# Two attentions recast by head pairs: half-array products for scores and values, in place of one head at a time

## The chip, the cores and the metric

The kernel runs on one core of a Trainium2 chip. The time is that of one execution on the device in microseconds (us); lower is better. The engines are named as the profile names them: PE is TensorE's matmul side and PEld its weight loads, DVE is VectorE, ACT is ScalarE, POOL is GpSimd, SP issues DMAs.

## The reference, cut to what matters

The program is a first block (gated delta rule, gated feed-forward) and a second block of two transformer layers over T = 528 positions, padded inside the reference to whole blocks. The change touches the two attentions of the second block, each with 16 heads of 64 elements. The first one masks keys by a selection of 128 of them (called DSA in the code), the second one has a decay (called fox). What each computes per head:

```
s = jnp.einsum('bqhd,bshd->bhqs', q[:, q0:q1], k[:, :q1]) * scale
s = jnp.where(causal, s + decay, -jnp.inf)      # DSA: selected keys instead of decay
p = jax.nn.softmax(s, axis=-1)
outs.append(jnp.einsum('bhqs,bshd->bqhd', p, v[:, :q1]))
...
return o.reshape(B, T, B_W) @ w_out
```

In DSA four query heads share a key and value head.

## The kernel before, in words

Everything is float32. The 528 positions are cut into five chunks of C = 106 (the last has 104): `ROWS` holds the chunk sizes, `ENDS` the ends 106, 212, 318, 424, 528. Heads come in pairs p = 0 to 7, and a pair's 2 x 64 elements fill the 128 partitions of one tile of `pf`. Large products around the attentions (`products`, L518) take each weight and each activation apart into a high and a low part (`xbh`, `xbl` for the attention's output) and run as fp32r.

An attention is 80 units, one for each head h and query chunk t (`unit(n)`); `pe_attention` is called once for DSA and once for fox, and so are `act_attention`, `dve_attention` and `pool_attention`. One unit goes through these steps:

- `scores(n)`, L2176: queries as weights, keys moving, one PSUM bank of up to 512 columns, or two of 264 for the last chunk. Since a matmul contracts over all 128 partitions, POOL has copied each head's half of the queries into `qz`, whose other half is zero (L2148, L2149). Then a mask (L2184) or the decay and the diagonal mask (L2179, L2181) is added by a bf16 product into the same bank.
- `top(n)` on DVE (L2276, L2280): the row maximum; `exp(n)` on ACT (L2245): the exponential with its row sum.
- `turn(n)`, L2194: PE transposes the probabilities, 106 columns at a time; `out(n)` on ACT (L2255, L2257) copies them from PSUM to `ptr`.
- `values(n)`, L2207: `ptr` as weights (106 columns), the head's 64 value columns moving; the output is tokens x 64.

After a head, DVE divides by the row sums into `otok` (L2288). After a pair, `turn_output(p)` (L2216) transposes the output on PE, and DVE splits it into `xbh` and `xbl` (L2298, L2301). PE, ACT and DVE each follow their own written order, tied by semaphores. PE's loop is: scores of unit n + 3, turn of unit n, values of unit n - 1. An fp32 matmul of the program stands in the profile as two PE instructions, each with its own weight load; they are called passes below. A transposition and a bf16 product are one pass.

The program states for every matmul which part of PE's array it uses. Before, all matmuls of the attentions use the whole array of 128 rows by 128 columns. Elsewhere some use a part: L2326, which sums squares between the products of the fox projections, uses 32 columns of it, and L1204, in the delta rule, 32 rows.

Of the kernel before, what the change touches and what calls it, by code (L numbers as in the profile page):

```python
# [24 lines left out]
P = 128  # L25
# [126 lines left out]
def build_program(nc, io):  # L152
# [134 lines left out]
    qz = r2("qz", [P, 4, T])  # L287
# [29 lines left out]
    prob = [rt(f"prob{u}", [C, T]) for u in range(3)]  # L317
    ptr = [rt(f"ptr{u}", [C, T]) for u in range(2)]
    otok = rt("otok", [C, 2, NCH, P])
    rowmax = rt("rowmax", [C, 2 * NCH])  # L320
    rowsum = rt("rowsum", [C, 2, NCH])
    rowinv = rt("rowinv", [C, NCH])
# [19 lines left out]
    def sem(name):  # L342
        return nc.alloc_semaphore(name)
# [24 lines left out]
    def both(name):  # L368
# [27 lines left out]
    at_q, at_s, at_mx = sem("att_q"), sem("att_scores"), sem("att_max")  # L396
    at_p, at_pt, at_pte, at_o, at_oe, at_ot, at_of = map(sem, (
        "att_prob", "att_prob_turned", "att_prob_out", "att_value", "att_value_out", "att_turned",
        "att_stored"))
# [1520 lines left out]
    def pool_dsa(pool):  # L1920
# [47 lines left out]
        zero_halves(pool)  # L1968
# [73 lines left out]
    def zero_halves(pool):  # L2042
        for i in range(0, 4, 2):
            pool.memset(qz[64:P, i, :], 0.0)
            pool.memset(qz[0:64, i + 1, :], 0.0)

# [51 lines left out]
    def unit(n):  # L2098

        h, k = divmod(n, NCH)  # L2100
        return h, ORDER[k]

    def att_banks(fox):

        at, held, plan = 2 * (SEGS["fox_out" if fox else "dsa_out"].b0 % 2), {}, {}

        def take(key, n):
            nonlocal at
            mine = [(at + x) % 4 for x in range(n)]
            plan[key] = mine[0], [held[x] for x in mine if x in held]  # L2110
            held.update((x, key) for x in mine)
            at += n

        for n in range(UNITS):
            if n > 2 * NCH and n % (2 * NCH) == NCH:
                take(("out", n // (2 * NCH) - 1), 2)
            take(("unit", n), 2 if unit(n)[1] == 4 else 1)
        take(("out", HEADS // 2 - 1), 2)
        return plan

    TURN_BANK = {0: 4, 1: 5, 2: 6, 3: 4, 4: 5}
    TURN_BACK = {0: 2, 1: 2, 2: 3, 3: 3, 4: 2}

    def scale_of(n):
        h, t = unit(n)
        return q_scale[0:ROWS[t], t, h:h + 1]
# [13 lines left out]
    def pool_attention(pool, fox):  # L2140
        call = att_call("pool")
        for p in range(HEADS // 2):
            x = tile_at(pf, p + 16 if fox else p)
            if fox:
                pool.wait_ge(f_app, p + 9)
            if p >= 2:
                pool.wait_ge(at_s, UNITS * call + 2 * NCH * (p - 1))
            pool.tensor_copy(qz[0:64, 2 * (p % 2), :], x[0:64])  # L2148
            pool.tensor_copy(qz[64:P, 2 * (p % 2) + 1, :], x[64:P]).then_inc(at_q, 1)  # L2149

    def pe_attention(pe, fox, begun=None):
        call = att_call("pe")
        v = vtok if fox else vt2
        plan = att_banks(fox)

        def banks_free(key):
            b, held = plan[key]
            units = [n for what, n in held if what == "unit"]
            outs = [n for what, n in held if what == "out"]
            if units:  # L2160
                pe.wait_ge(at_p, UNITS * call + max(units) + 1)
            if outs:
                pe.wait_ge(at_of, HEADS // 2 * call + max(outs) + 1)
            return b

        def scores(n):
            h, t = unit(n)
            p, hh = divmod(h, 2)
            rows = ROWS[t]
            b = banks_free(("unit", n))  # L2170
            if n % (2 * NCH) == 0:
                pe.wait_ge(at_q, HEADS // 2 * call + p + 1)
            key = (p if fox else p // 4 + 8) * T
            for x, (o, c) in enumerate(pieces(ENDS[t])):
                s = ps[0:rows, b + x, 0:c]
                pe.matmul(s, qz[:, 2 * (p % 2) + hh, t * C:ENDS[t]], pf[:, key + o:key + o + c], start=True, stop=False)  # L2176
                if fox:
                    diagonal = o + c == ENDS[t]
                    mm = pe.matmul(s, headrow[:, h, 0:rows], decay_row[:, o:o + c], start=False, stop=not diagonal)  # L2179
                    if diagonal:  # L2180
                        mm = pe.matmul(ps[0:rows, b + x, c - rows:c], ident16[0:rows, 0:rows],  # L2181
                                       mask16[0:rows, 0, 0:rows], start=False, stop=True)
                else:
                    mm = pe.matmul(s, ident16[0:rows, 0:rows], mask16[0:rows, t, o:o + c], start=False, stop=True)  # L2184
            mm.then_inc(at_s, 1)

        def turn(n):
            t = unit(n)[1]
            rows = ROWS[t]
            pe.wait_ge(at_p, UNITS * call + n + 1)  # L2190
            if n >= TURN_BACK[t]:
                pe.wait_ge(at_pte, UNITS * call + n - TURN_BACK[t] + 1)
            for kb in range(t + 1):
                mm = pe.transpose(ps[0:ROWS[kb], TURN_BANK[t] + kb // 4, (kb % 4) * rows:(kb % 4 + 1) * rows],  # L2194
                                  prob[n % 3][0:rows, kb * C:ENDS[kb]], ident[0:rows, 0:rows])
            mm.then_inc(at_pt, 1)

        def values(n):
            h, t = unit(n)
            p, hh = divmod(h, 2)  # L2200
            rows = ROWS[t]
            pe.wait_ge(at_pte, UNITS * call + n + 1)
            if n % NCH == 0 and h:
                pe.wait_ge(at_oe, HEADS * call + h)
            col = (p if fox else p // 4) * P + 64 * hh
            for kb in range(t + 1):
                mm = pe.matmul(ps[0:rows, 7, t * 64:(t + 1) * 64], ptr[n % 2][0:ROWS[kb], kb * rows:(kb + 1) * rows],  # L2207
                               v[0:ROWS[kb], kb, col:col + 64], start=(kb == 0), stop=(kb == t))
            if n % NCH == NCH - 1:
                mm.then_inc(at_o, 1)  # L2210

        def turn_output(p):
            pe.wait_ge(at_oe, HEADS * call + 2 * p + 2)
            b = banks_free(("out", p))
            for t in range(NCH):
                mm = pe.transpose(ps[:, b + t // 4, (t % 4) * C:(t % 4) * C + ROWS[t]], otok[0:ROWS[t], p % 2, t, :],  # L2216
                                  ident[0:ROWS[t], 0:ROWS[t]])
            mm.then_inc(at_ot, 1)

        if fox:  # L2220
            pe.wait_ge(acc_free, SEGS["fox_out"].b0)
        for n in range(3):
            scores(n)
        if begun is not None:
            begun(pe)
        for n in range(UNITS):
# [7 lines left out]
        values(UNITS - 1)  # L2234
        turn_output(HEADS // 2 - 1)

    def act_attention(act, fox):
        call = att_call("act")
        plan = att_banks(fox)

        def exp(n):
            h, t = unit(n)
            w_, rows = ENDS[t], ROWS[t]
            act.wait_ge(at_mx, UNITS * call + n + 1)
            act.activation(as_psum(prob[n % 3][0:rows, 0:w_], w_), psum_cols(plan["unit", n][0], rows, w_), ACT.Exp,  # L2245
                           bias=rowmax[0:rows, n % (2 * NCH):n % (2 * NCH) + 1],
                           accum_out=rowsum[0:rows, h % 2, t:t + 1],
                           **({} if fox else {"scale": scale_of(n)})).then_inc(at_p, 1)

        def out(n):  # L2250
            t = unit(n)[1]
            rows = ROWS[t]
            w_ = min(t + 1, 4) * rows
            act.wait_ge(at_pt, UNITS * call + n + 1)
            last = act.activation(ptr[n % 2][:, 0:w_], ps[0:C, TURN_BANK[t], 0:w_], ACT.Copy)  # L2255
            if t == 4:
                last = act.activation(ptr[n % 2][0:rows, w_:w_ + rows], ps[0:rows, TURN_BANK[t] + 1, 0:rows], ACT.Copy)  # L2257
            last.then_inc(at_pte, 1)

        exp(0)  # L2260
        exp(1)
        for n in range(UNITS):
            if n + 2 < UNITS:
                exp(n + 2)
            out(n)

    def dve_attention(dve, fox):
        call = att_call("dve")
        plan = att_banks(fox)

        def top(n):
            t = unit(n)[1]
# [590 lines left out]
```

## Time and profile before

| what | value |
|---|---|
| time, median of 3 runs | 2951.91 us (2951.75 to 2953.01) |
| profiled execution, its own time | 2949.52 us |
| its span, first to last instruction | 2947.7 us |
| PE busy in the span | 2743.1 us (93%) |
| DVE, ACT, POOL busy | 1416.6, 1027.5, 1097.4 us |
| DSA attention, from first scores to last values | about 1624.7 to 1769.5 us |
| fox attention | about 2384.9 to 2527.9 us |

The two attentions are some 288 us of the span together. In the profile a matmul's duration includes the way through the array; how fast matmuls follow each other is seen from starts alone, so the text below subtracts starts. A row with x8 is eight instructions in a run, with the start of the first.

### The profile page before, as it was taken

What the parts mean: (1) busy time and instruction counts of PE and PEld (TensorE: products, weight loads), DVE (VectorE), ACT (ScalarE), POOL (GpSimd) and SP (SyncE); (2) the same over time, 40 slices, a digit from 0 to 9 for tenths busy, and PEclk for the clock granted to TensorE, in tenths of its full rate; (3) what the DMA queues carried; (4) which work ended last, traced back from release to release, by engine and by line L of the source; (5) the groups of instructions that cost most, each with busy time, mean ns of one, the idle gap of its engine ahead of it and who ended that gap; (6) DMA issues with size and microseconds to landing.
All of it is one profiled execution on the core that took longest, in us unless ns stands there. A gap on an engine that the chain in (4) does not pass through costs nothing.

```text
span 2947.7 us, 48050 instructions
## 1 busy us (share of the span) xinstructions
PE 2743.1 (93%) x17591; PEld 2400.7 (81%) x17591; DVE 1416.6 (48%) x2151; ACT 1027.5 (35%) x1762; POOL 1097.4 (37%) x588
## 2 busy tenths in 40 slices
PE   6986888889999999999898899999999999999998
PEld 6964788868987778888778779999998988777876
DVE  2563565633213663323779556345366224555433
ACT  4762222233243332222433563212233255422221
POOL 3422433324444434444437104444444310344443
PEclk8997989999999999999999999999999999999999
DMA  3210000012333333333212002232322210133332
GB/s 97 90 50 7 11 10 12 11 59 89 92 89 93 93 94 92 93 93 94 86 43 65 1 1 81 91 86 86 93 86 79 65 30 1 58 93 93 93 93 93
DMA packets 88858, 197.89 MB, mean 67 GB/s; under 512 B 38140, under 2 KB 40238, under 8 KB 88728
## 3 DMA queue, kind: packets, MB, share of 16 engines
q1 hardware_dynamic: 84964, 192.72, 22.2%
q10 hardware_dynamic: 3764, 3.38, 0.4%
q8 instruction: 88, 1.44, 0.2%
q14 instruction: 42, 0.34, 0.0%
HBM read 192.24 MB, written 3.82 MB: 67 GB/s over the span
## 4 chain that ended last, share of the span: by engine, by line
issue 44%; PE 17%; POOL 12%; DVE 4%; ACT 1%; DVEq 1%; POOLq 1%; ACTq 0%
POOL wl L482 12%; PE ps L518 9%; PE ps L2176 2%; PE ps L2207 2%; DVE work L2076 1%; DVE top L2073 1%; PE ps L2194 1%; PE ps L1823 1%; PE ps L2326 1%; PE ps L2335 1%; ACT prob L2245 0%; POOLq L130 0%; DVE rowmax L2276 0%; PE ps L2179 0%; PE ps L893 0%
## 5 line engine op out<-in xcount | busy, mean ns | idle before, releaser
L482 POOL TENSOR_TENSOR wl<-wraw,wh 128x1024 fp32r<-128x1024 f32 x353 | 876.3, 2483 | 1289.8 <-ACT wh L474 1289.7
L474 ACT ACTIVATE wh<-wraw 128x1024 fp32r<-128x1024 f32 x353 | 372.6, 1055 | 576.7 <-PE ps L518 488.8
L518 PE MATMUL ps<-xah,wh 128*128 128x264 f32 (+1 forms) x2672 | 500.1, 328 | 25.6 <-ACT xah L847 14.2
L518 PE MATMUL ps<-xah,wl 128*128 128x264 f32 (+1 forms) x2672 | 488.3, 323 | 0.0
L518 PE MATMUL ps<-xal,wh 128*128 128x264 f32 (+1 forms) x2672 | 486.7, 322 | 0.0
L518 PEld LDWEIGHTS ps<-xah,wh 128*128 128x128 f32 x2672 | 405.7, 189 | 79.6 <-issue 23.2
L518 PEld LDWEIGHTS ps<-xah,wl 128*128 128x128 f32 x2672 | 404.0, 189 | 41.4 <-issue 0.8
L518 PEld LDWEIGHTS ps<-xal,wh 128*128 128x128 f32 x2672 | 402.3, 188 | 40.7
L666 DVE TENSOR_TENSOR res<-res,stage 128x512 f32 (+3 forms) x112 | 81.7, 729 | 440.8 <-ACT stage L582 440.8
L518 PE MATMUL ps<-xbh,wh 128*128 128x264 f32 (+1 forms) x1392 | 275.3, 338 | 13.5 <-POOL wl L482 12.9
L518 PE MATMUL ps<-xbh,wl 128*128 128x264 f32 (+1 forms) x1392 | 269.7, 333 | 0.0
L518 PE MATMUL ps<-xbl,wh 128*128 128x264 f32 (+1 forms) x1392 | 269.5, 333 | 0.0
L518 PEld LDWEIGHTS ps<-xbh,wh 128*128 128x128 f32 x1392 | 218.3, 189 | 48.5 <-POOL wl L482 16.4
L582 ACT ACTIVATE stage<-ps 128x512 f32<-128x512 f32 (+1 forms) x136 | 81.9, 603 | 466.9 <-PE ps L518 466.8
L518 PEld LDWEIGHTS ps<-xbh,wl 128*128 128x128 f32 x1392 | 217.7, 188 | 27.6
L518 PEld LDWEIGHTS ps<-xbl,wh 128*128 128x128 f32 x1392 | 217.5, 188 | 27.4
L659 DVE TENSOR_SCALAR xbh<-stage 128x512 f32 (+3 forms) x102 | 145.3, 1424 | 18.2 <-issue 16.6
L2176 PE MATMUL ps<-pf,qz 128*104 128x264 f32 (+4 forms) x384 | 125.3, 413 | 24.6 <-ACT prob L2245 13.7
L2276 DVE TENSOR_REDUCE rowmax<-ps 106x1 f32<-106x106 f32 (+4 forms) x160 | 77.7, 488 | 127.2 <-PE ps L2181 70.2
L661 DVE TENSOR_TENSOR xbl<-stage,xbh 128x512 f32 (+3 forms) x102 | 116.4, 1142 | 14.6
L1196 PE MATMUL ps<-xq,ob 106*106 106x106 f32 x480 | 65.4, 301 | 59.8 <-DVE xq L1499 39.9
L1196 PEld LDWEIGHTS ps<-xq,ob 106*106 106x106 f32 x480 | 60.7, 213 | 62.2 <-DVE xq L1499 41.5
(337 smaller groups left out, 3198.9 us busy)
## 6 DMA issues: line engine op xcount, KB each, us to landing
wraw<-in_w SPq DMA_DIRECT2D x353, 512.0 KB, 3.6
res<-in_x SPq DMA_DIRECT2D x4, 528.0 KB, 5.7
res<-in_x ACTq DMA_DIRECT2D x1, 2048.0 KB, 7.9
out<-res SPq DMA_DIRECT2D x1, 2048.0 KB, 6.9
block_in<-mt SPq DMA_DIRECT2D x120, 4.0 KB
xq<-block_out SPq DMA_DIRECT2D x120, 8.0 KB
block_out<-yy SPq DMA_DIRECT2D x20, 56.0 KB
cossin<-in_cossin ACTq DMA_DIRECT2D x1, 528.0 KB
```

The costliest lines, as they stand in the source:

```text
L474: act.activation(wh[:, s * DM:(s + 1) * DM], wraw[:, s * DM:(s + 1) * DM], ACT.Copy).then_inc(hi_done, 1)
L482: pool.tensor_tensor(wl[:, s * DM:(s + 1) * DM], wraw[:, s * DM:(s + 1) * DM], wh[:, s * DM:(s + 1) * DM].bitcast(F32), ALU.subtract).then ...
L518: mm = pe.matmul(ps[:, 2 * s + h, 0:width], ws[:, s * DM + kk * P:s * DM + (kk + 1) * P], x[:, at:at + width], start=(h not in [o[0] for o ...
L582: act.activation(shaped(out(j, u), live), acc(b, live=live), func, **more).then_inc(acc_free, 1)
L659: dve.tensor_scalar(hi, x, 1.0, None, ALU.mult)
L661: return dve.tensor_tensor(lo, x, hi.bitcast(F32), ALU.subtract)
L666: return dve.tensor_tensor(r, r, live_stage(u) if live else stage_at(u), ALU.add)
L1196: mm = pe.matmul(out_[:, sl], lhs(r, sl), rhs(r, sl), start=True, stop=True)
L1823: mm = pe.matmul(ps[0:ROWS[t], 4 + 2 * (n % 2) + x, 0:c], ix_zero[:, 2 * (m % 2) + hh, C * t:ENDS[t]], pf[:, 16 * T + o:16 * T + o + c], s ...
L2176: pe.matmul(s, qz[:, 2 * (p % 2) + hh, t * C:ENDS[t]], pf[:, key + o:key + o + c], start=True, stop=False)
L2207: mm = pe.matmul(ps[0:rows, 7, t * 64:(t + 1) * 64], ptr[n % 2][0:ROWS[kb], kb * rows:(kb + 1) * rows], v[0:ROWS[kb], kb, col:col + 64], s ...
L2276: most = dve.tensor_reduce(m, psum_cols(plan["unit", n][0], rows, w_), AX.X if w_ <= 512 else AX.XY, ALU.max, negate=True)
```

## The change

Both attentions are now 48 parts instead of 80 units. A part is a pair of heads and a query chunk; the last chunk is cut into key blocks 0 to 2 and 3 to 4, so that no part is wider than 424 columns. There are six parts per pair.

- Scores: no `qz`. Head 0 of the pair contracts over rows 0 to 63 of the array and head 1 over rows 64 to 127, each into a bank of its own. The mask and decay products still use the whole array.
- Values: the operands change places. The 64 value columns are the weights, and the turned probabilities move (106 columns); head 0 writes output partitions 0 to 63 and head 1 64 to 127, each from its half of the array's columns. The output comes out as heads x tokens, as the next stage needs it, so `otok` and `turn_output` go.
- The inverse row sums must then lie along the columns: `spread_sums` multiplies them, as 64 equal weight columns, with the identity matrix. ACT copies the result to `rowspread`, DVE multiplies (`store`), and POOL makes `xbh` and `xbl`.
- The copies of the turned probabilities are shared: ACT takes the first two key blocks of a part, DVE the rest. One `tensor_reduce` gives the maxima of both heads.

```diff
@@ parts @@
+    PARTS_OF = ((0, 0, 1), (1, 0, 2), (2, 0, 3), (3, 0, 4), (4, 0, 3), (4, 3, 2))
+    SCORE_BANK, TURN_BANK, VALUE_BANK = 0, 4, 6
@@ pool_attention @@
-            pool.tensor_copy(qz[0:64, 2 * (p % 2), :], x[0:64])
-            pool.tensor_copy(qz[64:P, 2 * (p % 2) + 1, :], x[64:P]).then_inc(at_q, 1)
+            x = ofull[p % 2][:, :]
+            pool.wait_ge(at_oe, 2 * (PAIRS * call + p + 1))
+            pool.tensor_copy(tile_at(xbh, p), x)
+            pool.drain()
+            pool.tensor_tensor(tile_at(xbl, p), x, tile_at(xbh, p).bitcast(F32), ALU.subtract).then_inc(at_of, 1)
@@ pe_attention @@
+        def scores(j):
...
+            if j >= 2:
+                pe.wait_ge(at_p, 2 * (ALL * call + j - 1))
...
+            for hh in range(2):
+                half = slice(64 * hh, 64 * hh + 64)
+                pe.matmul(ps[0:rows, b + hh, 0:hi - lo], pf[half, q0:q0 + rows], pf[half, k0 + lo:k0 + hi],
+                          start=True, stop=False)
...
-            for kb in range(t + 1):
-                mm = pe.matmul(ps[0:rows, 7, t * 64:(t + 1) * 64], ptr[n % 2][0:ROWS[kb], kb * rows:(kb + 1) * rows],
-                               v[0:ROWS[kb], kb, col:col + 64], start=(kb == 0), stop=(kb == t))
+        def spread_sums(p, i):
...
+                for hh in range(2):
+                    mm = pe.matmul(ps[64 * hh:64 * hh + 64, b, at:at + rows],
+                                   rowinv[0:rows, p % 2, t, hh:hh + 1].broadcast_to([rows, 64]),
+                                   ident[0:rows, 0:rows], start=True, stop=True)
...
+        def values(j):
...
+            for i, (kb, nk) in enumerate(groups(j)):
+                copied(pe, SLOT["turn", j, i], call)
+                for x in range(nk):
+                    for hh in range(2):
...
+                        mm = pe.matmul(ps[64 * hh:64 * hh + 64, VALUE_BANK + t // 4, at:at + rows],
+                                       v[0:n, kb + x, col:col + 64], ptr[TURN["turn", j, i] % 4][0:n, at2:at2 + rows],
+                                       start=(kb + x == 0), stop=(kb + x == t))
...
-        for n in range(UNITS):
-            if n + 3 < UNITS:
-                if n + 3 > 2 * NCH and (n + 3) % (2 * NCH) == NCH:
-                    turn_output((n + 3) // (2 * NCH) - 1)
-                scores(n + 3)
-            turn(n)
-            if n:
-                values(n - 1)
+        for j in range(ALL):
+            p, k = divmod(j, NS)
+            if j + 2 < ALL:
+                scores(j + 2)
+            turn(j)
+            if k == 4:
+                spread_sums(p, 0)
+            if k == 0 and p:
+                spread_sums(p - 1, 1)
+            if j and k != 4:
+                values(j - 1)
+            if k == 3:
+                values(j)
@@ dve_attention @@
+        def store(p, i):
...
+            dve.tensor_tensor(ofull[p % 2][:, lo:hi], ps[:, VALUE_BANK + i, 0:hi - lo], rowspread[:, lo:hi], ALU.mult
+                              ).then_inc(at_oe, 1)
```

PE's rows in the middle of the DSA attention before, from the scores of the fourth chunk of one head to the first scores of the next pair; `ps` is PSUM, `prob` the probabilities, `ptr` their transposed copies, and an x says how many matmuls of the program:

```order
L2176 MATMUL ps<-pf,qz 106x424
L2184 MATMUL ps<-mask_155,ident_156 106x424
L2194 MATMUL ps<-ident,prob_185 106x106
L2207 MATMUL ps<-vtok_dsa,ptr_187 104x64 x5
L2176 MATMUL ps<-pf,qz 104x264
L2184 MATMUL ps<-mask_155,ident_156 104x264
L2176 MATMUL ps<-pf,qz 104x264
L2184 MATMUL ps<-mask_155,ident_156 104x264
L2194 MATMUL ps<-ident,prob_183 106x106 x2
L2207 MATMUL ps<-vtok_dsa,ptr_186 106x64
L2216 MATMUL ps<-ident,otok 128x106 x4
L2216 MATMUL ps<-ident,otok 128x104
```

The same place in the changed kernel, where scores are L2193, masks L2205, turns L2223, spreads of the inverse sums L2234 and values L2254:

```order
L2193 MATMUL ps<-pf 106x424 x2
L2205 MATMUL ps<-mask_155,ident_156 106x424 x2
L2223 MATMUL ps<-ident,prob_183 106x106 x4
L2254 MATMUL ps<-ptr_186,vtok_dsa 64x106 x2
L2193 MATMUL ps<-pf 104x318 x2
L2205 MATMUL ps<-mask_155,ident_156 104x318 x2
L2223 MATMUL ps<-ident,prob_184 106x106 x6
L2254 MATMUL ps<-ptr_187,vtok_dsa 64x106 x4
```

The row of output transpositions is gone, every score and value product stands in twos, and PE goes through three uses of the array in each part: L2193 by row halves, L2205 and L2223 whole, L2254 (and L2234) by column halves. Further on in the same pair, at the fourth chunk and the last, the changed kernel has:

```order
L2223 MATMUL ps<-ident,prob_182 106x106 x8
L2254 MATMUL ps<-ptr_188,vtok_dsa 64x106 x4
L2254 MATMUL ps<-ptr_185,vtok_dsa 64x106 x2
L2254 MATMUL ps<-ptr_186,vtok_dsa 64x106 x4
L2254 MATMUL ps<-ptr_187,vtok_dsa 64x106 x4
L2193 MATMUL ps<-pf 106x106 x2
L2205 MATMUL ps<-mask_155,ident_156 106x106 x2
L2223 MATMUL ps<-ident,prob_183 106x104 x6
L2234 MATMUL ps<-ident,rowinv 64x106 x8
```

Here the values of the part that has just been turned (`ptr_186`, `ptr_187`) follow in the same round, behind those of the part before (`ptr_188`, `ptr_185`), and the spread takes the place of values in the round of the last chunk.

## Rows read from the trace of the kernel before

**Rows 1.** The page, section 5: the costliest group

```profile
L482 POOL TENSOR_TENSOR wl<-wraw,wh 128x1024 fp32r<-128x1024 f32 x353 | 876.3, 2483 | 1289.8 <-ACT wh L474 1289.7
```

**Rows 2.** Windows, one pair each of DSA and fox: PE, PEld, DVE, ACT, POOL, clock

```profile
1658.30:1676.00 17.70, 15.96 (x132) 13.44 (x131) 9.51 (x29) 10.64 (x33) 1.25 (x2) 1.00 0.00 1
2413.30:2430.40 17.10, 16.28 (x144) 13.94 (x143) 7.66 (x19) 9.86 (x32) 1.25 (x2) 1.00 0.01 2
```

**Rows 3.** Chain of waits in DSA, one same event three pairs apart

```profile
1640.53 0.88 ACT prob L2245 x2
...
1693.70 0.88 ACT prob L2245 x2
```

**Rows 4.** Chain of waits in fox, one same event four pairs apart

```profile
2413.33 0.53 PE ps L2207 x6
...
2481.73 0.53 PE ps L2207 x6
```

**Rows 5.** Timeline of PE in DSA: start, us, what, shapes, number

```profile
1758.43 0.61 PE L2194 MATMUL ps<-ident,prob 104*106 104x104 f32 x5
1758.88 0.88 PE L2207 MATMUL ps<-vtok_dsa,ptr 106*106 106x64 f32 x8
1759.59 0.91 PE L2176 MATMUL ps<-pf,qz 128*106 128x424 f32 x2
1760.34 0.34 PE L2184 MATMUL ps<-mask,ident 106*106 106x424 bf16 x1
1760.53 0.25 PE L2194 MATMUL ps<-ident,prob 106*106 106x106 f32 x1
```

**Rows 6.** Timeline of PEld, the weight loads, in the same stretch

```profile
1758.79 0.82 PEld L2207 LDWEIGHTS ps<-vtok_dsa,ptr 106*106 106x106 f32 x8
1759.54 0.27 PEld L2176 LDWEIGHTS ps<-pf,qz 128*106 128x106 f32 x2
```

**Rows 7.** Waits in the DSA attention: who for whom, us, times, longest

```profile
ACT ptr L2255 <- PE ps L2194: 36.5, 62, 0.9
...
PE ps L2176 <- ACT prob L2245: 8.1, 7, 1.2
```

**Rows 8.** Timeline of PE around L2326, which uses 32 columns

```profile
2239.58 0.77 PE L518 MATMUL ps<-xal,wh 128*128 128x264 f32 x5
2240.28 1.06 PE L2326 MATMUL ps<-fox_sq,win 128*16 128x264 f32 x4
2241.27 1.24 PE L518 MATMUL ps<-xah,wh 128*128 128x264 f32 x8
2242.34 1.13 PE L518 MATMUL ps<-xah,wl 128*128 128x264 f32 x8
2243.31 0.29 PE L518 MATMUL ps<-xal,wh 128*128 128x264 f32 x1
```

**Rows 9.** Timeline of PE around L1204, which uses 32 rows

```profile
449.64 1.69 PE L1204 MATMUL ps<-mt,ones 16*128 16x424 f32 x4
451.26 0.91 PE L1196 MATMUL ps<-rr,xq 106*106 106x128 f32 x6
```

**Rows 10.** Groups by shape in the DSA attention: busy us, mean ns, idle

```profile
L2245 ACT ACTIVATE prob<-ps,rowmax,q_scale 106x424 f32<-106x424 f32 x16 | 11.3, 705 | 8.2 <-DVE rowmax L2280 8.2
L2276 DVE TENSOR_REDUCE rowmax<-ps 106x1 f32<-106x424 f32 x16 | 9.6, 600 | 21.6 <-PE ps L2184 21.6
L2255 ACT ACTIVATE ptr<-ps 106x424 f32<-106x424 f32 x16 | 8.4, 526 | 2.3 <-PE ps L2194 2.3
```

**Rows 11.** Timeline where DSA begins

```profile
1623.24 0.62 POOL L2148 COPY qz<-pf 64x528 f32<-64x528 f32 x1 [7.59 <-DVEq L418]
1624.67 0.66 PE L2176 MATMUL ps<-pf,qz 128*106 128x106 f32 x2 [10.62 <-POOL qz L2149]
```

**Rows 12.** Timeline where fox ends

```profile
2527.45 0.68 PE L2216 MATMUL ps<-ident,otok 106*128 106x106 f32 x5 [0.85 <-DVE otok L2288]
2527.90 3.26 PE L518 MATMUL ps<-xbh,wh 128*128 128x512 f32 x7
```

More of the change, by code:

```diff
@@ new lines, in groups, with att_slots @@
+    def groups(j):
+        _, _, _, kb, nk = part(j)
+        return [(kb + i, min(2, nk - i)) for i in range(0, nk, 2)]
+    def att_slots():
+        slots, act, dve = [], 0, 0
+        for j in range(ALL):
+            p, k = divmod(j, NS)
+            mine = [("turn", j, i) for i in range(len(groups(j)))]
+            if k == 4:
+                mine.append(("spread", p, 0))
+            if k == 0 and p:
+                mine.append(("spread", p - 1, 1))
+            if j == ALL - 1:
+                mine.append(("spread", p, 1))
+            for key in mine:
+                on_dve = key[0] == "turn" and key[2] == 1
+                act, dve = (act, dve + 1) if on_dve else (act + 1, dve)
+                slots.append((key, on_dve, dve if on_dve else act))
+        return slots, act, dve
@@ new lines, in build_program, with slot_bank, copied, spread_tiles @@
+    SLOTS, ACT_COPIES, DVE_COPIES = att_slots()
+    SLOT = {key: n for n, (key, _, _) in enumerate(SLOTS)}
+    TURNS = [key for key, _, _ in SLOTS if key[0] == "turn"]
+    TURN = {key: n for n, key in enumerate(TURNS)}
+    def slot_bank(n):
+        return TURN_BANK + n % 2
+    def copied(e, n, call):
+        _, on_dve, count = SLOTS[n]
+        if on_dve:
+            e.wait_ge(at_td, DVE_COPIES * call + count)
+        else:
+            e.wait_ge(at_ta, ACT_COPIES * call + count)
+    def spread_tiles(i):
+        return range(4) if i == 0 else range(4, NCH)
@@ L2128, in pool_fox, with values_done @@
+    def values_done(j):
+        return sum(len(groups(i)) for i in range(j + 1))
+    ALL_GROUPS = values_done(ALL - 1)
     def pool_fox(pool):
@@ L2153, in pe_attention @@
         v = vtok if fox else vt2
[L2154 to L2176, printed above, removed]
+        def scores(j):
+            p, k, t, _, _ = part(j)
+            rows, (lo, hi) = ROWS[t], key_range(j)
+            b = SCORE_BANK + 2 * (j % 2)
+            if j >= 2:
+                pe.wait_ge(at_p, 2 * (ALL * call + j - 1))
+            if fox and k == 0:
+                pe.wait_ge(f_app, p + 9)
+            q0 = (p + 16 if fox else p) * T + t * C
+            k0 = (p if fox else p // 4 + 8) * T
+            for hh in range(2):
[3 more added lines that the diff above has]
+            for hh in range(2):
+                s = ps[0:rows, b + hh, 0:hi - lo]
@@ L2212, in turn_output, with slot_free @@
[L2212 to L2218, printed above, removed]
+        def slot_free(key):
+            n = SLOT[key]
+            if n >= 2:
+                copied(pe, n - 2, call)
+            return slot_bank(n)
@@ L2237, in act_attention @@
     def act_attention(act, fox):
         call = att_call("act")
[L2239 to L2258, printed above, removed]
+        def exp(j):
+            p, k, t, _, _ = part(j)
+            rows, (lo, hi) = ROWS[t], key_range(j)
+            act.wait_ge(at_mx, ALL * call + (j + 2 if k == 4 else j + 1))
+            if j >= 3:
+                act.wait_ge(at_t, turned_by(j - 3))
+            for hh in range(2):
+                h = 2 * p + hh
+                act.activation(prob[j % 3][0:rows, hh, 0:hi - lo], ps[0:rows, SCORE_BANK + 2 * (j % 2) + hh, 0:hi - lo],
+                               ACT.Exp, bias=rowmax[0:rows, (p * NCH + t) % 3, 0, hh:hh + 1],
+                               accum_out=rowsum[0:rows, p % 2, k, hh:hh + 1],
+                               **({} if fox else {"scale": q_scale[0:rows, t, h:h + 1]})).then_inc(at_p, 1)
@@ new lines, in turned_by, with out @@
+        def turned_by(j):
+            return len(SLOTS) * call + SLOT["turn", j, len(groups(j)) - 1] + 1
+        def out(j):
+            _, _, t, _, _ = part(j)
+            kb, nk = groups(j)[0]
+            n = TURN["turn", j, 0]
+            act.wait_ge(at_t, len(SLOTS) * call + SLOT["turn", j, 0] + 1)
+            wait(act, at_v, ALL_GROUPS * call + n - 3 if n >= 4 else 0)
+            w_ = 2 * nk * ROWS[t]
+            act.activation(ptr[n % 4][:, 0:w_], ps[0:C, slot_bank(SLOT["turn", j, 0]), 0:w_], ACT.Copy
+                           ).then_inc(at_ta, 1)
@@ L2260, in act_attention, with spread_out @@
+        def spread_out(p, i):
+            n = SLOT["spread", p, i]
+            act.wait_ge(at_t, len(SLOTS) * call + n + 1)
+            wait(act, at_oe, 2 * (PAIRS * call + p) - 1 + i)
+            lo, hi = (0, 4 * C) if i == 0 else (4 * C, T)
+            act.activation(rowspread[:, lo:hi], ps[:, slot_bank(n), 0:hi - lo], ACT.Copy).then_inc(at_ta, 1)
         exp(0)
         exp(1)
[L2262 to L2265, printed above, removed]
+        for j in range(ALL):
+            p, k = divmod(j, NS)
+            out(j)
+            if k == 4:
+                spread_out(p, 0)
+            if k == 0 and p:
+                spread_out(p - 1, 1)
+            if j + 2 < ALL and k != 2:
+                exp(j + 1 if k == 3 else j + 2)
+            if k == 3:
+                exp(j + 2)
@@ L2316, in build_program @@
+        for j in range(ALL):
+            p, k = divmod(j, NS)
+            if j + 2 < ALL:
+                top(j + 2)
+            if len(groups(j)) > 1:
+                out(j)
+            if k == 3:
+                invert(p, 0)
+            if k == 4:
+                store(p, 0)
+            if k == 5:
+                invert(p, 1)
+            if k == 0 and p:
+                store(p - 1, 1)
+        store(PAIRS - 1, 1)
     FOX = SEGS["fox"].b0
```

207 lines of the change are left out of this document (100 added, 107 removed).

## The prediction, made before the changed kernel ran

> **What bounds the kernel now.** I read the page first: PE is busy nearly all of the span, so a stage's time is PE's unless it waits. Then the windows, cut to one pair of heads. In DSA a pair takes 17.7 us, of which PE is busy 15.96; in fox 17.1 and 16.28 [rows 2]. DVE and ACT are busy 7.7 to 10.6 us of it. The clock is 1.00 in both, the 2.4 GHz level. The chain of waits gives the period exactly: 53.17 us for three pairs of DSA, 17.72 each, and 68.40 for four pairs of fox, 17.10 each [rows 3, 4]. The wait list of DSA has ACT waiting for turns by the dozen, and PE waiting for an exponential only 8.1 us in seven of its waits [rows 7]. PE sets both attentions, with small stalls.
>
> The timeline gives the price of a PE pass as the distance of starts [rows 5, 6]:
> - scores, 424 columns: 1759.59 to 1760.34, 0.75 for two passes, 0.375 each or 0.885 ns a column;
> - mask in bf16, 424 columns: 0.19, and 0.05 for 106;
> - turn: 1758.43 to 1758.88, 0.45 for five, 0.09 each;
> - values: only 64 columns move, but each pass takes 0.75/8 = 0.094 on PEld, from 1758.79 to 1759.54. The load of 106 fp32 weight columns sets it. By its columns a load of 64 would take 0.057, an estimate.
>
> A pair has 3176 score columns (two heads of 106 + 212 + 318 + 424 + 528) in two passes: 5.62 us. Masks 1.42, 30 turns 2.70, 60 value passes 5.63, five output turns 0.45. Sum 15.8 us; fox has ten diagonal masks more, 16.3. What is left of the periods, 1.9 and 0.8 us, is stall.
>
> **The change, part by part, for a pair.**
>
> Entering and leaving a part of the array. L2326 stands between fp32r products of 0.97/8 = 0.121 us each [rows 8]. Five of them from 2239.58 would end at 2240.19; L2326 starts 0.09 later. Its four passes of 264 columns, 0.222 to 0.234 each, end at 2241.17 to 2241.21; the next product starts 0.06 to 0.10 later, and its first eight take 1.07 instead of 0.97, since the first load lies open. L1204, in 32 rows, takes 1.62 us for four passes of 424 columns that make 1.50 at the rate above [rows 9]. So each change of use costs about 0.09 us and lays one weight load open. The new loop changes three times a round (columns to rows for the scores, rows to whole for masks and turns, whole to columns for values or spread), 18 times a pair: 18 x 0.09 = 1.62 us, plus the open loads. PE did none of this in the attentions before.
>
> The Trainium skill states the same (TensorEngine Tiling, "Key Properties"): changing the tiling mode drains TensorE. It speaks against this change, and the trace agrees with about 0.09 us. If switches were free, the sum would be 1.62 us a pair lower.
>
> Scores: 1588 columns per pass over the six parts, four passes (two heads, two each). What the trace of before does not show is two halves of the array at work together; no instruction there uses a second tile. Bounds: no overlap, four passes in a row; full overlap, two. Within a head the two passes share a half, so with matmuls started in program order A1, A2, B1, B2, only A2 and B1 can run together: three passes, 3 x 1.405 = 4.22, and six open loads of 0.094, 0.56. I take 4.8 (bounds 3.4 and 6.2; before 5.6).
>
> Masks: 1.42, and six open bf16 loads of 0.05: 1.7. Turns: 30, 2.7, unchanged.
>
> Values: still 60 passes. Now 106 columns move, 0.094 each, and 64 are loaded, 0.057. Alone a pass costs 0.094, as before: turning the operands around gains nothing by itself. With the halves overlapping, PE is held by the loads: 0.057. I take that, since it is the nearest row to a pass whose stream is hidden: 60 x 0.057 = 3.4, and six open loads, 0.3 (bounds: 0.047, half a stream, and 0.094; so 2.8 to 5.6).
>
> Spreads: five chunks, two heads, two passes, 20 x 0.057 = 1.1 (to 1.9). They replace output turns of 0.45: the product is fp32 and costs two passes where a turn costs one.
>
> Sum: 4.8 + 1.7 + 2.7 + 3.7 + 1.1 + 1.6 = 15.6 us, fox 16.1. The gain from overlap, about 1.4 in scores and 2.2 in values against passes in a row, is nearly eaten by switches, open loads and spreads.
>
> Other engines. ACT's 10.6 us a pair [rows 2] gain two short exponentials and the copy of the spread and lose a few copies of about 0.5 [rows 10]; DVE gives up splits and gets those copies, with half as many, wider maxima: the widest, 2 x 424 columns, is under twice 0.60 [rows 10]. Both stay near 10 of 16. POOL's subtraction of 528 columns is 2.48 x 528/1024 = 1.3 us [rows 1], its copy no more: idle time of POOL covers it; only at the end of an attention is it late, and there the first block of products leaves the last input tile for last.
>
> Stalls. `values` of the fourth chunk stands right behind its own turn. It needs the copy, 0.53 [rows 10] to 0.6 on DVE, while PE does values of the third chunk, six blocks, 12 passes x 0.057 plus a switch, 0.8: mostly covered, 0.2 open. Behind it on PE stand the next pair's scores. The other wait is scores of part j + 2 for the exponentials of part j. From the end of a part's scores to the end of its two exponentials the widest takes 1.2 + 0.16 + 2 x 0.9 = 3.2 us; PE has one and a half rounds, 3.9, to do meanwhile. Short rounds at a pair's start will stall. I take 1.1 us for DSA and 1.0 for fox, between the 0.8 and 1.9 of now.
>
> Periods: 16.7 us in DSA against 17.72, 8 x -1.0 = -8; 17.1 in fox against 17.10, nothing. The queries' copy into `qz` before the first scores of DSA, 1623.24 to 1624.67 [rows 11], goes: -1.3. At each end PE no longer waits for `otok`, 0.85 of idle time before the last output turns [rows 12], but waits some 0.3 for its last copies: -1.0 in all. Total -10.3. The profiled execution is 2949.5 us, 2.4 below the median of the runs; -10 from the median gives **2942 us**.
>
> **The rivals.**
>
> *Loads in program order (slower, 0.28).* A load in rows 6 starts as the matmul before it starts. If this is order, and not the one spare place for weights, then B's load waits for A2 to start: in the values a cycle of four passes is 0.094 + 0.057 + 0.094 + 0.057 = 0.30, 0.075 a pass, and each part's scores lose another load. 80 x 0.018 + 5 x 0.09 = 1.9 us a pair. PE then waits less, 0.6: 15.6 + 1.9 + 0.6 = 18.1 in DSA, 18.6 in fox. 8 x (0.4 + 1.5) = +15, less 2.3 at the ends, less up to 6 if short stalls vanish: +7 to +13, 2962 us. It decides once a pass of values is over some 0.065 us. For it speaks that no load in the trace is ever ahead of a matmul not yet started; against it, that in whole-array use the trace can't show it.
>
> A page rules near this: the Trainium skill (TensorE: Matmul & The Clock Gate, "The mechanism") has loads overlap running matmuls only where the row groups differ, and the column halves share all rows. Rows 6 contradict it in its bare form, since loads of 128 rows run under matmuls of 128 rows all through.
>
> *No overlap of halves (slower, 0.10).* Scores 6.2, values 5.6 + 0.3, spreads 1.9: 20.0 us with 0.6 of stall, and 20.5: +18 and +27, 2995 us. Nothing in the profile speaks against it. The Trainium skill does (TensorEngine Tiling, "Key Properties"): tiles load and multiply in parallel.
>
> *The halves run by themselves (faster, 0.16).* If each half takes up its passes without regard to the other's, scores are two passes, 3.4, and values 0.047: 13.4 us of work. Then the chain from scores to exponentials (3.2 us for two rounds of 2.3) and ACT start to hold: 15.4 to 15.7 us. 8 x (-2.2 - 1.5) = -30, 2920 us.
>
> *The new wait is not covered (0.08).* Copies queued behind two exponentials on ACT (1.8 us) come late for values of the fourth chunk: 1 us in each of 16 pairs, 2958 us.
>
> **How the numbers follow.** Chances: forecast 0.36, the rivals 0.28, 0.10, 0.16, 0.08, something else 0.02. The forecast's own range is 2934 to 2950. From 2914 (the independent halves) to 2975 (program order, with its upper bound) all but no overlap is in; that leaves about 0.13 out. A measurement can tell about 0.2%, 6 us. Faster by more: most of the forecast, 0.29, and the independent halves, 0.16: 0.45. Within: 0.18. Slower by more: 0.37.
>
> **What the changed profile would show.** Starts of values (L2254) 0.057 us apart right, 0.075 program order, 0.094 no overlap. Scores of 424 columns: from the first start to the mask 1.1 to 1.2 us right, 1.5 no overlap, 0.75 independent. PEld idle about 0.09 before each change of use. Pairs at 16.7 and 17.1 us. PE's wait for copies before L2254 small, POOL late nowhere. The prediction is wrong above all if the halves overlap more or less than that, or if a switch between halves costs more than the 0.09 of a part in 32 columns.

## The result, and the profile after

The changed kernel takes 2907.68 us (median of 4 runs, 2903.69 to 2911.96), the kernel before 2952.06 us beside it (4 runs, 2951.75 to 2953.01). The ratio is 0.985, 95% interval 0.9838 to 0.9862: 44 us faster, far more than the forecast 10, and 6 us below the range. The profiled execution took 2911.96 us, the slowest of the four; its span is 2910.1 us, so 37.6 of the 44 us can be looked for in it.

Windows of the changed kernel, one pair of DSA and one of fox; columns as in [rows 2]:

```profile
1685.05:1699.22 14.17, 13.53 (x149) 9.24 (x147) 7.47 (x20) 10.51 (x33) 1.93 (x2) 1.00 0.01 2
2430.41:2444.61 14.20, 13.77 (x158) 9.73 (x156) 6.74 (x15) 9.48 (x33) 1.93 (x2) 1.00 0.00 1
```

A pair now lasts 14.17 and 14.20 us, 3.55 and 2.90 less than the periods of [rows 3, 4]. PE still fills it (13.53 and 13.77), so PE still sets both attentions; PE itself has less to do. The chain of waits, here POOL's last step of a pair in DSA and in fox, says the same, 14.17 to 14.25 a pair:

```profile
1678.57 1.31 POOL xbl L2175
1692.82 1.30 POOL xbl L2175
1706.99 1.31 POOL xbl L2175
...
2438.40 1.31 POOL xbl L2175
2452.60 1.30 POOL xbl L2175
```

PE's timeline in the middle of a DSA pair. To be read by starts, and beside [rows 5]: scores L2193, mask L2205, turns L2223, spreads L2234, values L2254.

```profile
1688.78 0.76 PE L2254 MATMUL ps<-ptr,vtok_dsa 106*64 106x104 f32 x12
1689.46 0.79 PE L2193 MATMUL ps<-pf 64*106 64x318 f32 x4
...
1690.99 0.53 PE L2254 MATMUL ps<-ptr,vtok_dsa 106*64 106x104 f32 x8
1691.46 0.96 PE L2193 MATMUL ps<-pf 64*106 64x424 f32 x4
1692.35 0.56 PE L2205 MATMUL ps<-mask,ident 106*106 106x424 bf16 x2
1692.75 0.53 PE L2223 MATMUL ps<-ident,prob 106*106 106x106 f32 x4
1693.21 0.40 PE L2254 MATMUL ps<-ptr,vtok_dsa 106*64 106x106 f32 x4
1693.54 0.79 PE L2193 MATMUL ps<-pf 64*104 64x318 f32 x4
```

Scores of 424 columns: 1691.46 to 1692.35, 0.89 for four passes and the change of use behind them. Without that change (0.09) it is 0.80, near the 0.75 that the prediction had named for independent halves and far from its own 1.1 to 1.2. Values that stand between turns and scores: twelve passes take 0.68 to the next scores, four 0.33, so eight more cost 0.35, or 0.044 each, where the prediction had 0.057.

Four narrow windows on the values (L2254) just after 1680.94, PE busy and, as (x..), the passes under way in each (a pass stays under way for 0.25 to 0.31 us, so the number grows):

```profile
1680.94:1681.03 0.09, 0.08 (x2) 1.00 0.00 0
1681.03:1681.12 0.09, 0.09 (x4) 1.00 0.00 0
1681.12:1681.21 0.09, 0.09 (x6) 1.00 0.00 0
1681.21:1681.30 0.09, 0.09 (x8) 1.00 0.00 0
```

Every 0.09 us two more passes are under way, not one: each half runs at the 0.094 of [rows 6] for itself, side by side with the other. That is the price of 0.045 a pass.

What waits now, DSA attention (us in total, times, longest):

```profile
POOL xbh L2173 <- DVE ofull L2378: 114.7, 8, 31.8
DVE rowmax L2343 <- PE ps L2205: 39.4, 41, 2.8
...
ACT ptr L2308 <- PE ps L2223: 11.2, 18, 1.5
...
PE ps L2234 <- ACT ptr L2308: 3.6, 8, 0.6
PE ps L2193 <- ACT prob L2292: 2.8, 7, 1.5
...
PE ps L2254 <- DVE ptr L2361: 0.5, 2, 0.3
```

POOL, DVE and ACT wait for PE. PE waits about 0.43 us a pair for the copy ahead of the spreads and 0.2 for exponentials; values wait for their copies twice in the stage.

Where it is not faster: the start of fox. Timeline of PE there, and windows of the first two pairs and of the stretch at the low clock:

```profile
2367.83 1.40 PE L2193 MATMUL ps<-pf 64*106 64x318 f32 x4 [3.58 <-ACT prob L2292]
```

```profile
2361.98:2384.12 22.14, 18.57 (x111) 11.96 (x111) 5.51 (x10) 11.66 (x39) 0.00 (x0) 0.59 0.00 1
2384.12:2402.01 17.89, 17.63 (x158) 12.35 (x156) 6.83 (x15) 8.70 (x29) 1.93 (x2) 0.75 0.00 1
2366.00:2390.00 24.00, 21.91 (x130) 14.68 (x131) 5.88 (x11) 10.40 (x35) 0.00 (x0) 0.50 0.00 1
```

PE stands idle for 3.58 us until the first exponentials are there, and then the granted clock is 0.50, the 1.2 GHz level, for 24 us and more. The first two pairs, from first scores to first scores, take 22.14 and 17.89 us, 11.6 us more than two steady pairs. (Before, the first fox pair took 17.08 us with a wait of 2.30 in it, as long as a steady one.)

The stages, from first scores to the first product of what follows, before from [rows 11, 12] and the table of times before, after from the starts 1627.68, 1746.44, 2361.98 and 2491.74 of these lines:

```profile
1627.68 0.69 PE L2193 MATMUL ps<-pf 64*106 64x106 f32 x4 [9.17 <-DVEq L417]
...
1746.44 1.12 PE L517 MATMUL ps<-xbh,wh 128*128 128x264 f32 x7
...
2491.05 0.40 PE L2234 MATMUL ps<-ident,rowinv 104*64 104x104 f32 x4 [0.47 <-DVE rowinv L2371]
2491.25 0.56 PE L2254 MATMUL ps<-ptr,vtok 106*64 106x104 f32 x8
2491.74 1.89 PE L517 MATMUL ps<-xbh,wh 128*128 128x512 f32 x7
```

DSA took about 144.8 us and now takes 118.8 (-26); fox took 143.0 and now takes 129.8 (-13).

### The profile page after: what moved, and what is told of

Its sections match the earlier page's. It is cut to its first block, busy times and chain, and to the rows that moved or that the text cites. A ratio compares the mean times of both kernels' runs of the same rounds, so it can differ in the third digit from the quotient of the medians.

```text
span 2910.1 us, 48627 instructions
## 1 busy us (share of the span) xinstructions
PE 2717.8 (93%) x17831; PEld 2342.6 (80%) x17831; DVE 1397.0 (48%) x2063; ACT 1023.8 (35%) x1762; POOL 1106.1 (38%) x584
## 3 DMA queue, kind: packets, MB, share of 16 engines
q8 instruction: 90, 1.47, 0.2%
## 4 chain that ended last, share of the span: by engine, by line
issue 53%; POOL 13%; PE 5%; DVE 3%; POOLq 3%; DVEq 1%; ACT 0%; ACTq 0%
POOL wl L481 12%; PE ps L517 3%; POOLq L2166 2%; DVE work L2069 1%; DVE top L2066 1%; PE ps L1822 1%; POOL xbl L2175 1%; POOLq L130 0%; POOLq L2174 0%; PE ps L892 0%; PE ps L880 0%; POOLq L2163 0%; PE ps L2193 0%; DVEq L618 0%; DVEq L2067 0%
## 5 line engine op out<-in xcount | busy, mean ns | idle before, releaser
L517 PE MATMUL ps<-xah,wh 128*128 128x264 f32 (+1 forms) x2672 | 500.4, 328 | 24.0 <-ACT xah L846 14.2
L658 DVE TENSOR_SCALAR xbh<-stage 128x512 f32 (+3 forms) x102 | 146.3, 1434 | 18.9 <-issue 17.3
L2343 DVE TENSOR_REDUCE rowmax<-ps 106x2 f32<-106x212 f32 (+2 forms) x96 | 68.0, 708 | 96.0 <-PE ps L2202 48.8
L2173 POOL CAST xbh<-ofull 128x528 fp32r<-128x528 f32 x16 | 10.0, 625 | 233.9 <-DVE ofull L2378 233.9
```

What stands on the lines that cost most here:

```text
L517: mm = pe.matmul(ps[:, 2 * s + h, 0:width], ws[:, s * DM + kk * P:s * DM + (kk + 1) * P], x[:, at:at + width], start=(h not in [o[0] for o ...
L658: dve.tensor_scalar(hi, x, 1.0, None, ALU.mult)
L2343: most = dve.tensor_reduce(rowmax[0:rows, n, 1 if k == LAST4 else 0, :], ps[0:rows, b:b + 2, 0:hi - lo], AX.X, ALU.max, negate=True)
```

## The experiments

Three readings of the result are weighed. The main one: the halves of the array run wholly by themselves, in scores and in values, and that is what the forecast missed; 0.09 us a change of use holds. Rival one: only one of the two overlaps, and the rest comes from work that left. Rival two: the changes of use cost nothing, and the halves overlap only in part. (The expectations letter their own theories anew each time.) The last experiments look at the fox start instead. Steady pairs are taken from the chain of waits, POOL's last step of a pair. All experiments start from the changed kernel.

**Values in one half.** Both heads' values go through column half 0 and are summed there, so nothing can overlap; the second head's output is left out.

```diff
-                        mm = pe.matmul(ps[64 * hh:64 * hh + 64, VALUE_BANK + t // 4, at:at + rows],
+                        mm = pe.matmul(ps[0:64, VALUE_BANK + t // 4, at:at + rows],
...
-                                       start=(kb + x == 0), stop=(kb + x == t))
+                                       start=(kb + x == 0 and hh == 0), stop=(kb + x == t and hh == 1))
```

> Both heads' value products go to the column half 0 and are summed there, so the second head's output is left out; number, shapes and order of the instructions and all changes of use of the array stay. Theory A, the two halves run side by side and that is the gain: 30 passes of 0.09 us a pair come back on the path, 16 x 2.7 = +43, 2951 us. Theory B, the forecast's partial overlap limited by loads: +14 to +28. Theory C, the gain is from fewer waits between the engines: within 5 us of the changed kernel.

Measured: 2945.83 us (10 runs, 2941.98 to 2949.25), ratio to the kernel before 0.998 (0.997 to 0.9989); pairs of 16.36 and 16.87 us, +2.19 and +2.67. Timeline of PE, the longest run of values in a DSA pair:

```profile
1703.52 2.76 PE L2254 MATMUL ps<-ptr,vtok_dsa 106*64 106x106 f32 x28
1706.20 0.44 PE L2193 MATMUL ps<-pf 64*106 64x106 f32 x4
```

and the same 28 passes in the changed kernel, in fox:

```profile
2485.79 1.50 PE L2254 MATMUL ps<-ptr,vtok 106*64 106x106 f32 x28
2487.22 0.75 PE L2223 MATMUL ps<-ident,prob 104*106 104x104 f32 x6
```

2.68 us against 1.43, less 0.09 for the change behind each: 0.0925 and 0.048 a pass. Without the overlap of the values the kernel is 38 us slower, near the +43 of both halves side by side and outside the +14 to +28 of a partial overlap.

**Scores in one half.** Both heads contract over rows 0 to 63, so the second head's scores are those of the first.

```diff
-                half = slice(64 * hh, 64 * hh + 64)
+                half = slice(0, 64)
```

> Both heads' scores contract over rows 0 to 63, so the second head's scores are those of the first head; all else as it is. Theory A: two more passes of each part's width in a row, 2 x 1.32 us a pair, +42, 2950 us, less what stalls take up. Theory B (program order, only the second pass of head 0 beside the first of head 1): +21. Theory C: within 5 us.

Measured: 2981.98 us (4 runs, 2970.44 to 2985.97), ratio 1.0095 (1.0068 to 1.0122); pairs of 16.74 and 16.84, +2.57 and +2.64. Timeline of PE, the scores of 424 columns:

```profile
1731.11 1.67 PE L2193 MATMUL ps<-pf 64*106 64x424 f32 x4
1732.71 0.56 PE L2205 MATMUL ps<-mask,ident 106*106 106x424 bf16 x2
```

1.60 us where the changed kernel has 0.89: four passes of 0.375 and one change of use. The pairs make 16 x 2.6 = 42 us, as expected. Rival one falls: each of the two overlaps costs about 40 us when it is taken away. A pair with neither would take 14.17 + 2.19 + 2.57 = 18.9 us in DSA and 14.20 + 2.67 + 2.64 = 19.5 in fox, an estimate, and so more than before (17.72 and 17.10): the overlap carries the whole gain. The run lost not 42 but 74 us. The windows of its profile show where most of the other 32 lie:

```profile
1618.00:1706.00 88.00, 81.11 (x376) 52.31 (x378) 26.53 (x71) 31.03 (x92) 3.84 (x4) 0.50 0.00 1
1706.00:1740.00 34.00, 32.87 (x308) 22.83 (x304) 15.16 (x40) 20.78 (x63) 3.85 (x4) 0.99 0.01 1
```

The granted clock is 0.50 for 88 us at the start of DSA, and pairs there take up to 29.6 us. Why this order of work keeps the clock low for so long is not settled.

**Values head by head.** Within a group all passes of head 0, then all of head 1, instead of taking turns.

```diff
-                for x in range(nk):
-                    for hh in range(2):
+                for hh in range(2):
+                    for x in range(nk):
```

> Values of a group of two key blocks are written head by head (four passes of half 0, then four of half 1) instead of alternating. Theory A, each half takes up its own matmuls as they come: no change, at most +3 us. Theory B, matmuls start in the order of the program and overlap only with the neighbour: of eight passes only two overlap in each group, +25 to +30 us.

Measured: 2909.81 us (4 runs, 2902.45 to 2913.52), ratio 0.9852 (0.9833 to 0.9871); pairs of 14.22 and 14.31, +0.05 and +0.11. Its 28 passes of values in a row:

```profile
2412.25 1.55 PE L2254 MATMUL ps<-ptr,vtok 106*64 106x106 f32 x28
2413.72 0.44 PE L2193 MATMUL ps<-pf 64*106 64x106 f32 x4
```

They take 1.47 us with the change behind them, where taking turns took 1.43. Even four passes of one half in a row leave the other half running: a half takes up its passes ahead of matmuls that were issued earlier for the other. Starts in program order, on which two of the prediction's cases rested, would have cost 25 to 30 us by the expectation; 2 were measured.

**More changes of use**, and **the same product without them.** Between masks and turns of each part stands a tiny product of 64 columns: in the first kernel in a column half, which adds two changes a part, in the second in the whole array, which adds none. (The second one's weights are 128 columns, the first one's 64.)

```diff
+                if i == 0:
+                    pe.matmul(ps[0:64, b, 0:64], ident[:, 0:64], ident[:, 0:64], start=True, stop=True)
```

```diff
+                if i == 0:
+                    pe.matmul(ps[:, b, 0:64], ident[:, :], ident[:, 0:64], start=True, stop=True)
```

> Between masks and turns of each part stands one more tiny product of 64 columns by a column half, so the use of the array changes twice more (96 parts). By 0.09 us a change with the loads laid open and two passes: 0.39 us a part, +38 us against the changed kernel, and 17 more than the control in the whole array. If changes cost nothing by themselves: no more than the control.

> The control: the same tiny product over the whole array, so the use does not change there. Two passes with loads of 128 columns, 0.107 us each: 0.21 us a part, +20 us. The difference of the two is the price of two changes in each of 96 parts, 17 us by 0.09 each.

Measured: with changes 2958.18 us (10 runs, 2944.03 to 2967.25; ratio 1.0012, 0.9994 to 1.0031), pairs of 16.15 and 16.57; without 2923.88 (4 runs, 2918.2 to 2932.06; 0.9914, 0.9891 to 0.9936), pairs of 15.02 and 15.52. Timelines of PE around one such product (L2221), with changes and then without:

```profile
1738.18 0.56 PE L2205 MATMUL ps<-mask,ident 106*106 106x424 bf16 x2
1738.68 0.33 PE L2221 MATMUL ps<-ident 128*64 128x64 f32 x2
1738.94 0.57 PE L2225 MATMUL ps<-ident,prob 106*106 106x106 f32 x4
```

```profile
1738.48 0.56 PE L2205 MATMUL ps<-mask,ident 106*106 106x424 bf16 x2
1738.88 0.33 PE L2221 MATMUL ps<-ident 128*128 128x64 f32 x2
1739.05 0.53 PE L2225 MATMUL ps<-ident,prob 106*106 106x106 f32 x4
```

The mask takes 0.50 to the next start with a change and 0.40 without, the product 0.26 and 0.17. Per pair the difference is 1.13 and 1.05 us for 12 changes, 0.09 each. Rival two falls. The 0.10 ahead of the product is free of the difference in weights; in the 0.09 behind it the wider loads of the control are not told apart. (The times differ by 34 us, twice the 17 of the pairs; the kernel with changes has a window around its fox start, 2360 to 2425, at a mean clock of 0.72.)

**Products in the wait at the fox start.** Fifteen products whose result is not used stand where PE waits for the first exponentials.

```diff
+            pe.wait_ge(f_app, 16)
+            for _ in range(15):
+                pe.matmul(ps[:, VALUE_BANK, 0:HT], ident[:, :], pf[:, 0:HT], start=True, stop=True)
```

> In the changed kernel fox begins with a wait of PE for the first exponentials, 3.5 us, and the clock then stands at 0.50 for some 27 us; its first two pairs take 22.2 and 17.9 us instead of 14.2. Here 15 useless products of 264 columns fill that wait (they write a bank that the values write over later). Theory: the halved clock took most of what fox gained less than DSA. It expects the clock at 1.00 all through fox's start, the second pair at 14.2 us, and 2898 us (8 to 11 less than the changed kernel). Rival: the start is slow because of ACT's copies and table load, and the clock costs nothing: no change, within 2 us.

Measured: 2906.36 us (4 runs, 2902.11 to 2909.65), ratio 0.9845 (0.9829 to 0.9862). In its profile the low clock is gone, windows over the start of fox:

```profile
2362.00:2380.00 18.00, 17.85 (x140) 13.12 (x139) 5.41 (x11) 11.20 (x35) 0.00 (x0) 1.00 0.01 4
2380.00:2400.00 20.00, 19.14 (x225) 13.53 (x222) 8.82 (x21) 13.70 (x49) 1.93 (x2) 1.00 0.00 1
```

but the median moved by only 1.3 us, within the spread, where 8 to 11 had been expected. So it was run again beside an unchanged copy, with one more kernel that also fills the idle time before DSA (24 such products into bank 4, ahead of the barrier and behind ACT's last copy of the values).

> The changed kernel once more, word for word, to stand beside the next two on the same chip. Its first fox pairs took 22.15 and 17.89 us instead of 14.20 in the profiled execution, under a granted clock of 0.50 for 27.3 us. Theory A (that spell belongs to most executions): 2904 to 2912 again. Theory B (the spell comes in some executions and not in others): single times scattered over the same range of some 8 us, and a profile in which the spell may be absent.

> The first experiment again (15 useless products of 264 columns in TensorE's wait at the start of the fox attention). Theory A (the clock spell belongs to most executions of the changed kernel and the products take it away): 5 to 8 us below the unchanged kernel beside it, and first pairs of about 17.8 and 14.2 us. Theory B (the spell is not in every execution, or moves elsewhere): within 2 us of it.

> As the one before, and 24 useless products of 264 columns (about 0.29 us each, some 7 us) in TensorE's idle stretch of 9 us before the first scores of the DSA attention. If a granted clock of 0.50 at the start of the DSA attention comes from that idle stretch, the first DSA pair falls from 14.8 us to about 14.2 and the stretch at 0.50 is gone or shorter: 1 to 3 us below the experiment beside it. If the clock there is set by something else, no difference, and if the products end late, up to 1 us more.

Measured, all on one chip: unchanged 2908.41 us (4 runs, 2906.93 to 2911.95; ratio 0.9851, 0.9836 to 0.9866), fox filled 2903.78 (5 runs, 2900.52 to 2905.41; 0.983, 0.9817 to 0.9844), both filled 2907.03 (5 runs, 2905.41 to 2909.49; 0.9845, 0.9832 to 0.9858). Windows over the first stretch of fox in the unchanged copy:

```profile
2362.00:2380.00 18.00, 14.27 (x78) 8.13 (x75) 4.12 (x7) 9.96 (x31) 0.00 (x0) 0.63 0.02 7
2380.00:2400.00 20.00, 19.51 (x212) 14.56 (x210) 8.60 (x21) 12.06 (x42) 1.92 (x2) 0.90 0.01 2
```

The low clock is there again, but shorter (0.90 in the second window against a mean of 0.75 in the second pair of the first profile). Its length differs between executions, which fits the scatter of the unchanged kernel's times. Over both batches the unchanged kernel has a mean of 2908.3 (8 runs) and the filled one 2904.6 (9 runs): 4 us, between the two theories (5 to 8 us, or under 2).

The filling was too long to show the whole price of the clock. In the first experiment's profile the products and what follows them are

```profile
2364.71 6.84 PE L2267 MATMUL ps<-pf,ident 128*128 128x264 f32 x30
2371.48 0.79 PE L2193 MATMUL ps<-pf 64*106 64x318 f32 x4
```

Its first scores start at 2362.60, so the third part's scores come 8.88 us later. In the changed kernel they come 5.85 us after the first (2361.98 to 2367.83), when the exponentials are there. So 3.0 us of the products stand behind the end of the wait. The first fox pair with them takes 17.78 us, at a clock of 1.00; without these 3.0 us it would take 14.75, an estimate. By that the low clock costs (22.14 - 14.75) + (17.89 - 14.20) = 11.1 us in the first profile of the changed kernel and 21.61 - 14.75 = 6.9 in the second, of which the filling gave back 8.1 and 3.8. A shorter filling was not run.

Filling the DSA start did not pay: 3 us slower than the kernel with fox alone filled, where 1 to 3 us faster had been expected. The first scores came at 1631.84 instead of 1628.96 us, while the first pair shrank only from 15.00 to 14.27. By then DVE had long been waiting for PE:

```profile
1631.86 0.08 DVE L2386 MEMSET rowsum<- 106x24 f32 x1 [5.70 <-PEq L417]
```

The expectation had 7 us for the 24 products; they are 48 passes of 264 columns, and by the 6.77 us of the 30 above they need 10.8 even at full clock. So the expected gain was not tested fairly.

## Why the prediction was wrong

**The step that failed.** "Within a head the two passes share a half, so with matmuls started in program order A1, A2, B1, B2, only A2 and B1 can run together: three passes." Four passes take the time of two: 0.80 us for 424 columns, and 1.51 (1.60 less 0.09) as soon as both heads share a half. The program order binds only passes of the same half; values head by head cost 0.05 to 0.11 us a pair more, where one order of starts would have cost 25 to 30 us in all. It shows in the scores too: program order there is both passes of head 0, then both of head 1, and still the four take the time of two. Two cases, the forecast and the slower rival, took one order of starts for all of PE. The Trainium skill (TensorEngine Tiling, "Key Properties") says that tiles load and multiply in parallel; this case's rows agree, and go as far as two of everything at once.

**The same step in the values.** "With the halves overlapping, PE is held by the loads: 0.057." The loads of the two halves also run side by side, so a pass costs half of its own stream, 0.045 to 0.048.

By terms, a DSA pair, from the starts in one pair of the changed kernel, each with the change of use that follows it:

| term | forecast | measured |
|---|---|---|
| scores and 6 changes | 4.8 + 0.5 | 3.77 |
| masks | 1.7 | 1.60 |
| turns and 6 changes | 2.7 + 0.5 | 3.36 |
| values, spreads and 6 changes | 3.7 + 1.1 + 0.5 | 4.8 |
| stalls | 1.1 | 0.64 |
| pair | 16.7 (the terms, rounded, 16.6) | 14.17 |

Scores account for 1.5 of the missed 2.5 us, values for 0.5, stalls for 0.5.

**The rival that was right, and its size.** "The halves run by themselves" had 13.4 us of work; 13.53 were measured. Its 15.4 to 15.7 us a pair added 2.0 to 2.3 us of stalls that did not come. It reasoned that the chain from scores to exponentials takes 3.2 us and holds PE up in each round of 2.3. But short parts and long parts follow each other, PE runs two parts ahead, and the list of waits has only 2.8 us for exponentials in the whole of DSA (7 waits). Had its stalls been 0.6, it would have given 14.0 and, with the half microsecond of fox's diagonal masks, 14.5 us a pair, 8 x (-3.7 - 2.6) = -50 us less the clock's share, and the range would have reached down to the result. In the no-overlap rival the sum is off: its terms add up to 20.0 without the 0.6 of stall, so 20.6 and 21.1, +55 and not +45. The passes at 0.048 rule that rival out either way.

**Right.** The direction. A change of use costs 0.09 us (1.13 and 1.05 us for 12). Turns have the forecast price. Spreads seem to, but by luck: 20 passes take 1.10 us with a change of use in it, so 0.05 each as in the values, not 0.057. The new wait, values of the fourth chunk behind their own turn, is covered: 0.5 us in all of DSA. POOL is late only at an attention's end, and the products there start at once. DVE and ACT are busy 6.7 to 10.5 of 14.2 us. The 1.3 us for the copies of the queries can't be seen: nine profiles with the same code ahead of DSA (the changed kernel, its copy and all experiments but the one with both starts filled) start DSA between 1623.54 and 1629.31, the kernel before at 1624.67.

**Not foreseen.** The start of fox. Before, the scores of four units stood ahead of PE's wait for the first exponentials, and it lasted 2.30 us:

```profile
2390.58 0.30 PE L2194 MATMUL ps<-ident,prob 106*106 106x106 f32 x1 [2.30 <-ACT prob L2245]
```

Now two parts stand ahead of it, PE waits 3.58 us, and the clock stays at 0.50 for far longer: windows of 4 us show 0.81 and 0.77 there before, and then 1.00 again. The steady pairs promise 8 x 3.55 + 8 x 2.90 = 51.6 us. The stages gave 26 + 13 = 39: fox fell 10 us short, about what the low clock at its start took (11.1, the estimate above), and DSA 2.4, its first pair (14.77 us) at a low clock too. The span shows 37.6, since DSA started 3.0 us later than before and 1.4 came back behind fox. Part of that late start may be a low clock in code that the change doesn't touch: in a window at 612 to 624 us the changed kernel's profiled execution has a granted clock of 0.76 and the kernel before 1.00; the unchanged copy has 0.86 and the two profiles with fox filled 1.00 and 0.83, so it differs between executions of the same code.

## What to carry to other kernels

Where a matmul contracts over 64 rows or writes 64 outputs, put two of them in the two halves of the array: the pair then costs what one did, even for fp32 with its two passes and even when the halves are not issued in turns. Group the work by use of the array, since each change costs 0.09 us; 18 changes here cost 1.6 us against 5 us of overlap. And look at what stands before the first dependent wait of a stage: an idle TensorE of 3.6 us was followed here by 17 to 27 us at half clock (worked out from the means of the windows). Filling such a wait pays only if the filling ends with the wait: here it ran 3.0 us over, and 4 us were left of 7 to 11.

## What the runs showed of the hardware

- The two halves start passes 0.09 us apart each, and at the same time as one another; one half's passes overtake those issued earlier for the other (28 passes of values head by head take 1.47 us, taking turns 1.43, in one half 2.68).
- In whole-array use a load of all 128 rows runs beside a running matmul of all rows. In the kernel before, eight loads are busy for 1.04 us beside the matmuls of [rows 8], which start 0.121 us apart and are busy from 2242.34 on without a break:

```profile
2242.22 1.04 PEld L518 LDWEIGHTS ps<-xah,wl 128*128 128x128 f32 x8
```

  So do loads in column halves, which share all rows: 28 passes of values in 1.43 us are 0.051 us each, and a load of theirs lasts 0.136. The Trainium skill (TensorE: Matmul & The Clock Gate, "The mechanism") lists loads as overlapping only where row groups differ; the rows here do not bear that out.
- How long the granted clock stays low after PE's idle time differs from one execution to the next: at the fox start it fell after the same 3.6 us of idle time in both profiles of the changed kernel, with two slow pairs in one (22.14 and 17.89 us) and one slow pair (21.61) in the other. With both heads' scores in one half it lasted 88 us at the DSA start. What sets the length is not settled here.
